# A two-block transformer kernel: the first attention moves between half chunks of the input projections, and sixteen modulation chunks become VectorE dot products

## The reference, cut to what matters

```python
# first block, one layer; x [256, 1024], ctx [256, 1024], float32
sh1, sc1, g1, sh2, sc2, g2 = split(silu(c) @ w_mod + b_mod, 6)       # w_mod [1024, 6144]
csh1, csc1, ...            = split(silu(c_ctx) @ w_mod + b_mod, 6)   # only the first two are used
hc = rmsnorm(ctx, n1) * (1 + csc1) + csh1;  kc, vc = hc @ w_in[:, KV]
h  = rmsnorm(x, n1) * (1 + sc1) + sh1
q, k, v, gb, gc, u, ga, gv = split(h @ w_in)                         # 4352 columns
y_attn = windowed_attention(rope(q), rope(k), v, kc, vc, sink) @ w_attn_out      # 8 heads of 64
y_conv = (gb * short_conv(gc * u)) @ w_conv_out
x = x + g1 * ((sigmoid(ga) * y_attn + sigmoid(gv) * y_conv) @ w_mix_out)
h2 = rmsnorm(x, n2) * (1 + sc2) + sh2
x = x + g2 * peer(h2, ...)      # per token 8 heads x 16 of 16384 experts: 128 rows of u and v gathered
# second block: two layers of attention and conv-gated FFN on x, then a norm
```

## Time and profile before

| | |
|---|---|
| median of three runs | 1725.31 us (1717.51 to 1727.1) |
| profiled execution | 1723.54 us, span 1721.3 us |
| PE busy | 1512.4 us (88%) |
| DVE, ACT, POOL busy | 1051.7, 771.6, 274.8 us |
| mean granted PE clock | 0.959 |
| DMA | 431.76 MB, mean 251 GB/s |

### The profile page before, as it was taken

The page is one execution under the profiler, slowest core; times in us unless marked ns, Lnnn a source line. Parts: engine busy times, 40 slices in busy tenths (PEclk is TensorE's granted clock), DMA queues, the critical chain, the costliest instruction groups (busy, mean ns, idle before and its releaser), DMA issues.

```text
span 1721.3 us, 22861 instructions
## 1 busy us (share of the span) xinstructions
PE 1512.4 (88%) x8364; PEld 1105.5 (64%) x8364; DVE 1051.7 (61%) x2111; ACT 771.6 (45%) x1648; POOL 274.8 (16%) x260
## 2 busy tenths in 40 slices
PE   7999998699888798877777779898999897899997
PEld 3897577554444233322222269788999886899997
DVE  4664335656666666766665557526777666367774
ACT  2644423244444344444444353536555546445553
POOL 0000000244344344344444200000000000000000
PEclk9999999899999999999999989789999998899998
DMA  8345344599999999999999924204555430145541
GB/s 359 138 157 182 137 172 147 234 405 420 419 419 420 420 420 420 420 420 419 420 420 420 392 89 160 99 30 147 190 174 192 165 128 26 74 172 172 193 172 73
DMA packets 59986, 431.76 MB, mean 251 GB/s; under 512 B 6784, under 2 KB 7296, under 8 KB 7552
## 3 DMA queue, kind: packets, MB, share of 16 engines
q0 software_dynamic: 36864, 268.45, 37.7%
q1 hardware_dynamic: 22320, 161.62, 26.0%
q10 hardware_dynamic: 720, 0.62, 0.1%
HBM read 429.62 MB, written 1.05 MB: 250 GB/s over the span
## 4 chain that ended last, share of the span: by engine, by line
PE 44%; DMA 23%; ACT 6%; DVE 6%; issue 2%; POOL 0%; ACTq 0%; POOLq 0%; DVEq 0%; SPq 0%
DMA arena<-in_peer_uv,experts 19%; PE banks L612 18%; PE banks L968 10%; PE banks L1074 7%; DMA tok_b<-in_peer_uv,experts 2%; DVE wlow L1527 2%; PE banks L854 2%; PE banks L644 1%; ACT diag L1347 1%; PE banks L828 1%; ACT scores L1255 1%; PE banks L666 1%; DVE arena L1912 1%; ACT whigh L1116 1%; ACT L1339 1%
## 5 line engine op out<-in xcount | busy, mean ns | idle before, releaser
L968 PE MATMUL banks<-arena,diag 128*128 128x512 f32 x824 | 402.0, 624 | 102.2 <-ACT diag L1347 101.6
L1912 DVE CUSTOM_DVE_ANT_0 arena<-arena,scores 128x1024 f32<-128x1024 f32 x206 | 252.5, 1226 | 191.4 <-DMA arena<-in_peer_uv,experts 189.6
L968 PEld LDWEIGHTS banks<-arena,diag 128*128 128x128 f32 x824 | 148.9, 194 | 342.0 <-ACT diag L1347 206.4
L1527 DVE TENSOR_TENSOR wlow<-wring,whigh 128x1024 fp32r<-128x1024 f32 x234 | 275.5, 1220 | 109.6 <-ACT whigh L1116 109.5
L1489 POOL DMA_INDIRECT arena<-in_peer_uv,experts x206 | 220.6, 1071 | 627.6 <-DVE experts L1876 322.3
L1116 ACT ACTIVATE whigh<-wring 128x1024 fp32r<-128x1024 f32 x234 | 233.8, 1048 | 140.3 <-DMA wring<-in_w_down 33.2
L612 PE MATMUL banks<-f_high,whigh 128*128 128x256 f32 x720 | 206.3, 287 | 17.2 <-DVE f_low L1563 11.8
L612 PE MATMUL banks<-f_low,whigh 128*128 128x256 f32 x720 | 205.2, 285 | 0.0
L612 PE MATMUL banks<-f_high,wlow 128*128 128x256 f32 x720 | 205.1, 285 | 0.0
L1339 ACT ACTIVATE dots<-dots 128x1 f32<-128x1 f32 x256 | 51.5, 201 | 302.2 <-DVE dots L1912 301.5
L612 PE MATMUL banks<-a_high,whigh 128*128 128x256 f32 x560 | 166.9, 298 | 14.2 <-DVE a_low L1535 7.9
(11 more groups left out here) (237 smaller groups left out, 2470.5 us busy)
## 6 DMA issues: line engine op xcount, KB each, us to landing
wring<-in_w_up SPq DMA_DIRECT2D x44, 1024.0 KB, 4.9
wring<-in_w_down SPq DMA_DIRECT2D x22, 1024.0 KB, 4.8
wring<-in_w_in SPq DMA_DIRECT2D x17, 1024.0 KB, 5.3
wring<-in_w_mod SPq DMA_DIRECT2D x16, 1024.0 KB, 4.8
wring<-in_w_qkv_a SPq DMA_DIRECT2D x12, 1024.0 KB, 4.9
arena<-in_w_mod SPq DMA_DIRECT2D x8, 1024.0 KB, 15.8
wring<-in_peer_w_q SPq DMA_DIRECT2D x8, 1024.0 KB, 7.3
wring<-in_w_mix_out SPq DMA_DIRECT2D x4, 1024.0 KB, 4.9
```

The source lines that it names most:

```text
L968: mm = nc.tensor.matmul(banks[:, 2 + 2 * b + half, :], diag[:, n % DIAGS, :], ring[n % RING][:, D + half * 512:D + (half + 1) * 512], star ...
L1527: V.tensor_tensor(low, w, high.bitcast(F32), ALU.subtract).then_inc(w_split, 1)
L1912: V.tensor_tensor_reduce(out=ring[n % RING][:, 0:D], in0=ring[n % RING][:, 0:D], in1=h2tok[:, b, :], scale=1.0, scalar=0.0, op0=ALU.mult, ...
```

## The change

The twelve modulation chunks of the attention and the four of the gather are gone from SP, PE and ACT. In their place the host lays the remaining 4096 columns of `w_mod` out by feature (`w_mod_t`: a row for each output feature) and `c` in 128 equal rows. POOL loads 32 tiles of 128 x 1024 (0.5 MB) into four buffers, and DVE multiplies each with the SiLU of the row of `c` and sums along it (`dot_tile`, one fused instruction, which leaves one column of `mod`): 24 tiles in the slots 7 to 30 of the new loop, 8 in the output products. `c` comes by a DMA of 0.5 MB among the early chunks; its SiLU is on ACT before the first norm's root.

The projections and the first attention are one loop of 32 slots on PE, ACT and DVE. A slot is half a chunk's product (24 matmuls); group n of the attention begins at slot 10 + 2n: score in that slot, turn two slots later, weigh four later, turn back six later. The scores of each group use banks 2 and 3 alone, and projections banks 0 and 1. The maxima become one fused instruction for each head, instead of two for scale and mask and one reduction. ACT now copies the gates plainly and makes their eight sigmoids after the loop. The first chunks of `w_qkv_a` wait until the last row of the gather has landed.

```diff
-MODS_PE = [i for i in range(MOD_TILES // 2) if i not in MODS_DVE]
-ROWS_1 = MODS_EARLY - len(MODS_DVE)
-ROWS_2 = 5 * KT // 2 - len(MODS_DVE)
-ROWS_3 = len(MODS_PE)
+MODS_PE = [i for i in range(MODS_EARLY) if i not in MODS_DVE]
+DOT_TILES = list(range(2 * KT, 3 * KT)) + list(range(4 * KT, 5 * KT)) + list(range(3 * KT, 4 * KT)) + list(range(5 * KT, 6 * KT))
+DOTS_MIXED = 3 * KT
+ROWS_1 = len(MODS_PE)
...
-MOD_ROWS = [88, 96, 104, 112]
...
+        dot_tiles = [region(4, 56 * T), region(4, 60 * T), hT[:, 0:4, :], hT[:, 4:8, :]]
+        dot_tiles = [t.rearrange("p k t -> p (k t)") for t in dot_tiles]
+        z_high, z_low = c_high[:, 0:4, :], c_low[:, 0:4, :]
+        o_high, o_low = c_high[:, 4:8, :], c_low[:, 4:8, :]
...
+        TURN, WEIGH, BACK = 2, 4, 6
+        FIRST_SLOT = 10
...
+                plan["at"] = {FIRST_SLOT + 2 * n: g for n, g in enumerate(groups)}
+                plan["slots"] = max(plan["at"]) + BACK + 2
...
-        add_mods(ROWS_1, ROWS_2)
...
+            load_mod(3)
+            sp.dma_start(c_row, a["c_rows"]).then_inc(c_row_in, 16)
+            for i in range(4, MODS_EARLY):
...
-                        sp.wait_ge(row_used, ROWS - 5)
+                        sp.wait_ge(row_in[(ROWS - 1) % RING], 16 * ((ROWS - 1) // RING + 1))
...
+            plan = plans[0]
+            for slot in range(plan["slots"]):
+                i, j = divmod(slot, 2)
+                if slot == 2:
+                    for which in range(2):
+                        key_value(which, 0)
+                        key_value(which, 1)
+                if i < 16:
+                    if j == 0 and i >= 2:
+                        pe.wait_ge(proj_read, i - 1)
+                    mm = tile_pair(i % 2, in_chunks[i + 1], high_low[0], (h_ready, 0) if slot == 0 else None, only=(j,))
+                    if j == 1:
+                        mm.then_inc(proj_made, 1)
+                if slot == 5:
...
+                if slot == FIRST_SLOT:
+                    pe.wait_ge(dup_read, 2)
+                    pe.wait_ge(kv_read, 3)
+                    pe.wait_ge(roped, 3)
+                at = plan["at"]
+                if slot - BACK in at and at[slot - BACK]["last"]:
+                    turn_heads(at[slot - BACK])
+                if slot - WEIGH in at:
+                    weigh(plan, at[slot - WEIGH])
+                if slot - TURN in at:
+                    turn_probs(at[slot - TURN])
+                if slot in at:
+                    score(plan, at[slot])
...
-                if n in MOD_ROWS:
-                    mod_chunk(ROWS_2 + MOD_ROWS.index(n))
...
+                    act.wait_ge(c_row_in, 16)
+                    nc.scalar.activation(c_row, c_row, ACT.Silu).then_inc(c_row_ready, 1)
...
+                if j == 1 and i < 16:
+                    if i == 1:
+                        act.wait_ge(kv_made, 1)
+                        copy(kraw, banks[:, 3, :]).then_inc(kv_read, 1)
+                        act.wait_ge(kv_made, 2)
+                        copy(kv_turned, banks[:, 6, :]).then_inc(kv_read, 1)
+                    dst, part = dests[i]
+                    act.wait_ge(proj_made, i + 1)
+                    copy(flat(dst[:, 2 * part:2 * part + 2, :]), banks[:, i % 2, :]).then_inc(proj_read, 1)
+                    if i == 3:
+                        for g in range(2):
+                            act.wait_ge(dup_made, g + 1)
+                            copy(kdup1[:, g, :], banks[:, 3 + g, :]).then_inc(dup_read, 1)
+                        act.wait_ge(kv_made, 3)
+                        copy(v1.rearrange("p b n -> p (b n)"), banks[:, 5, :]).then_inc(kv_read, 1)
+                    if i == 5:
+                        act.wait_ge(angles_ready, 1)
+                        nc.scalar.activation(sin2[:, :], tmp[:, 0, 0:T], ACT.Sin)
+                        nc.scalar.activation(cos2[:, :], tmp[:, 0, T:2 * T], ACT.Sin).then_inc(tables_ready, 1)
+                at = plan["at"]
+                if slot - BACK in at and at[slot - BACK]["last"]:
+
+                    act.wait_ge(z_made, 1)
+                    heads_out(plan, at[slot - BACK])
+                if slot - TURN in at:
+                    probs_out(at[slot - TURN])
+                if slot in at:
+                    exps(at[slot])
+                if j == 1 and i < 16:
+                    round_next()
+                if slot == 21:
+                    act.wait_ge(z_made, 1)
+                    copy(flat(z_high), flat(zconv[:, :, :])).then_inc(z_rounded, 1)
+            act.wait_ge(proj_read, 16)
+            for d in (sg_a, sg_c):
+                for part in range(4):
+                    tiles = flat(d[:, 2 * part:2 * part + 2, :])
+                    nc.scalar.activation(tiles, tiles, ACT.Sigmoid).then_inc(gates_ready, 1)
+
+            round_next()
...
+            for n, tile in enumerate(DOT_TILES):
+                if n == 0:
+                    pool.wait_ge(mod_rows, ROWS_1)
+                if n == 2:
+                    pool.wait_ge(h_ready, normed(1, 0))
+                if n >= 4:
+                    pool.wait_ge(tile_used, n - 3)
+                pool.dma_start(dot_tiles[n % 4], a["w_mod_t"][(tile - 2 * KT) * P:(tile - 2 * KT + 1) * P, :]
+                               ).then_inc(tile_in[n % 4], 16)
...
+            def dot_tile():
+
+
+                n = next(dot_next)
+                w = dot_tiles[n % 4]
+                dve.wait_ge(tile_in[n % 4], 16 * (n // 4 + 1))
+                V.tensor_tensor_reduce(out=w, in0=w, in1=c_row, scale=1.0, scalar=0.0, op0=ALU.mult, op1=ALU.add,
+                                       accum_out=mod[:, DOT_TILES[n], 0:1]).then_inc(tile_used, 1)
...
+                for j in range(heads):
+                    at = (j % each) * width
+                    ins = V.tensor_tensor_reduce(
+                        out=scores[:, n % 2, j * width:(j + 1) * width],
+                        in0=banks[:, g["score_bank"] + j // each, at:at + width], in1=g["mask"], scale=SCALE,
+                        scalar=LOWEST, op0=ALU.add, op1=ALU.max, accum_out=top[:, n % 2, j:j + 1])
+                ins.then_inc(score_read, 1)
...
+            for slot in range(5, plan["slots"]):
+                i, j = divmod(slot, 2)
+                if slot == 5:
+                    rope_key()
+                if slot == 6:
+                    rope_query(0)
+                    rope_query(1)
+                at = plan["at"]
+                if slot - BACK - 1 in at and at[slot - BACK - 1]["last"]:
+                    low_out(plan, at[slot - BACK - 1])
+                if slot - WEIGH in at and at[slot - WEIGH]["last"]:
+                    dve.wait_ge(tables_ready, 1)
+                    normalise(at[slot - WEIGH])
+                if slot in at:
+                    maxima(at[slot])
+                if j == 1 and i < 16:
+                    low_next()
+                if slot == 9:
+                    dve.wait_ge(roped, 3)
+                    angles()
+                if slot == 16:
+                    conv_middle()
+                if slot == 17:
+                    conv_left()
+                if slot == 18:
+                    conv_right()
+                if slot == 20:
+                    conv_out()
+                if slot == 23:
+                    low_conv()
+                if 7 <= slot < 7 + DOTS_MIXED:
+                    dot_tile()
...
+            dve.wait_ge(tile_used, DOTS_MIXED)
+            mixed = mod[:, 2 * KT:5 * KT, 0]
+            step.link(V.tensor_tensor(mixed, mixed, vcol[:, V_BMOD + 2 * KT:V_BMOD + 5 * KT], ALU.add))
             dve.sem_inc(mod_ready, 1)
             step.link(gains(2, 4, 0, V_N2))
 
 
             for g in range(8):
                 dve.wait_ge(mix_made, g + 1)
+                dve.wait_ge(gates_ready, g + 1)
                 sl = slice(2 * (g % 4), 2 * (g % 4) + 2)
                 if g < 4:
                     V.tensor_tensor(flat(merged[:, sl, :]), banks[:, g, :], flat(sg_a[:, sl, :]),
                                     ALU.mult).then_inc(mix_read, 1)
+                    dot_tile()
+                    dot_tile()
...
+    arrays["w_mod_t"] = np.ascontiguousarray(inputs["w_mod"][0][:, 2 * D:].T)
+    arrays["c_rows"] = np.ascontiguousarray(np.tile(inputs["c"], (P, 1)))
...
```

More of the change, by code:

```diff
@@ L98 @@
 C_END = C_MASK + 10 * P
+ALIGN = 8
 V_C = 0
@@ L461, in build @@
         len_of_ring = [0]
-        mod_chunks, in_chunks = [], []
-        def add_mods(first, last):
-            for p in range(first, last):
-                mod_chunks.append(add(chunk_of(a["w_mod"], MODS_PE[p]), (mod_rows, p + 1), split=False))
-        def mod_bank(p):
-            if p >= ROWS_2:
-                return 6
-            return 7 if ROWS_1 <= p else p % 2
+        in_chunks = []
         in_order = [1, 0] + list(range(2, len(W_IN_CHUNKS)))
@@ new lines, in _, with exps @@
+                dests += [(d, part) for part in range(4)]
+            def exps(g):
+                width = g["blocks"] * P
```

(10 more changed lines are left out.)

468 lines of the change are left out of this document (232 added, 236 removed).

## The result

The changed kernel takes 1659.2 us (median of 4 runs, 1653.3 to 1663.7), the kernel before 1721.4 (4 runs, 1717.3 to 1727.1): ratio 0.9635, 95% interval 0.9607 to 0.9663. It is 62 us faster; I had said 50.5, and my range ended at 1665. The forecast of 1675 counted from 1725.3, the median of the three runs that I had seen, and the kernel before has 1721.4 in the four runs here. So 3.9 of the 15.8 us between 1675 and 1659.2 are that base, and 11.7 are gain that I had not forecast. The profiled execution took 1661.6 (span 1659.8).

The account below looks back on a forecast made before the run. PE bounds projections and first attention, almost half of the latter's PE work not attention; DMA bounds the gather. Gains 46.9 - 8.1 + 10.0 + 3.2 = 52.0, less 1.5 for hops, 50.5 us: forecast 1675, range 1665 to 1692.

Parts of the forecast that it names:

- Modulation leaves PE, cover, stalls: Projections and first attention: modulation off PE -45.1 us, waits covered -3, new stalls +3.3; gain given as 46.9.
- my two small terms: Projections and first attention: about 3 us of waits at the stage's ends go, 3.3 us of stalls come.
- The one wait: First attention group: PE could transpose at 102 us but waits 2 to 3 us for late exponentials.
- The output products become DVE's: Output products: 12.4 us to the first merge, then 27.5 on DVE, 39.9 against 31.8; 8.1 us given back.
- The head, the tiles' DMAs: Early chunks and tile loads: the added load of c, its SiLU and 32 tile loads cost nothing.
- The gather stage: Gather: four chunks leave it, each worth one row of 2.48 us; -10.0 us.
- the signs: What would show the forecast right; in the gather an unchanged period of 2.5 and a length 10 us shorter.
- The end of the gather: Gather's end: the next projection's first chunks are issued after the last row, so the sums' copy starts 3.2 us earlier.
- Semaphore hops: Some forty new changes between product kinds: 1.5 us taken off the gain.
- The splits did not fall behind: Mixed stage rival: PE waits for weight splits, 2 us per pair over eight pairs, 1691; chance 0.15.
- the gather's gain came: Gather rival: the gain does not come and the late issue costs what it saves, 1688; chance 0.07.
- the clock: Mixed stage rival: PE at half clock, +74 us, about 1749; chance 0.03 together with anything else that loses.

Follow-up runs that it names:

- e12: The changed kernel with seven sigmoids before the last half chunk, eight dot tiles moved into the mixed slots, and the angles in slot 6, not 9: 1641.3 us.
- e6: The changed kernel with seven of the eight sigmoids moved ahead of the last half chunk: 1650.4 us.
- e7: The changed kernel with the last eight dot tiles moved out of the output products, into the pairs of slots with attention: 1649.4 us.
- e5: The changed kernel with four 1 MB loads of w_mod put back into the gather, read by nothing: 1666.4 us.
- e2: The changed kernel without its eight unused floats, so all buffers behind them start 32 bytes lower: 1665.5 us.
- e1: The kernel before with only eight unused floats (32 bytes a partition) put ahead of its buffers: 1707.7 us.
- e4: The changed kernel with the next projection's first three loads issued five rows ahead of the gather's end again: 1659.0 us.
- e8: The changed kernel with the first attention moved behind the last half chunk (first slot 32 instead of 10): 1677.7 us.
- e11: The changed kernel with seven sigmoids moved ahead of the last half chunk and the last eight dot tiles moved among the mixed slots: 1649.2 us.

## Why the prediction was wrong, step by step

- **Modulation leaves PE, cover, stalls (46.9):** near the 47.7 measured, partly by luck. The terms that I listed, -45.1 - 3 + 3.3, make 44.8 and not 46.9; no row gives the 2.1 between them. The windows from 46 us on have PE busy 45.2 us less (187.5 before, 142.3 after), which is my 45.1, and idle 2.5 us less (6.1 before, 3.6 after), where my two small terms together gave 0.3 more. The projections before had 3.0 us of idle time of their own, which I did not count. The one wait was predicted as 2 to 3 us near 102 and is 2.17 before 104.62; e12 removed it, and the loss of clock behind it, which my term did not hold.
- **The output products become DVE's (8.1 given back):** right, 8.7. The chain that I gave for the first merge (12.4 us) was right in length, but not in what bounds it: e6 shows that the sigmoids hide a late load of about the same end. e7 shows the rest, 17.5 us without dots where I had 27.5 - 9.8 = 17.7.
- **The head, the tiles' DMAs (0):** right. The first projection matmul starts at 45.6, and DVE waited once for a tile, 1.59 us.
- **The gather stage (-10.0): the step that failed.** I wrote that "a row takes 2.48 us" and in the signs "an unchanged period of 2.5". So I priced four rows fewer and held the period of the other 256 fixed; the pad in the diff stood in my sum at nothing, without a reason. The four chunks are worth what I said (9.5 in e5). But the period fell to 2.44, because 32 unused bytes put the buffers on a multiple of 256: 10.7 us by e2, 11.2 by e1. With 11 for it, the sum of the gain is 61.5, against 62.2 measured; counted from 1721.4 that is 1660.
- **The end of the gather (-3.2):** right in the trace, 3.8 in e4; the times can't confirm it.
- **Semaphore hops (1.5 taken off):** 3.1 went behind the gather, but that stretch varies by 11 us between executions of the same instructions, so nothing can be said of this term.
- **The rivals:** the splits did not fall behind (e7 bears even 8 dots more); the gather's gain came; the clock was 0.99 in the mixed stage, with 1.00 everywhere but behind the one wait (0.89 from 95 to 110), and e8 shows half speed for the attention's pieces alone. The gather's rate is no part of any rival: I had none for a faster row.

## What to carry to other kernels

Price every line of a diff that moves an address, not only those that move work: here one stage is bound by DMA for 650 us, and a pad of 32 bytes gave 1.6% of its rate, 11 us. Work in small pieces with a dependent chain (attention) is best laid between long products even when PE could do it alone: the waits are covered and the clock is kept, and in e8's trace each was about half of what the other order lost. Take work off the engine that ends a stage by name: the sigmoids beside a late load were worth 3 us, the dots on DVE's chain 7.5.

## What the runs showed of the hardware that I had not expected

- Gathered rows of 8 KB into SBUF (the on-chip memory in which the buffers lie): 427 GB/s with buffers that start at a multiple of 256 bytes of a partition, 421 at 64 or 128 beyond one, 419 to 420 at 224.
- One wait of 2.17 us of PE was followed by some 3.5 us at half speed (e11), and the same wait by none in e2, e4, e6 and e7. One of 7.2 us ahead of transposes, scores and weighings brought the granted clock to 0.50, and it stayed there for some 25 us of unbroken work of that kind: transposes of 8 blocks took 1.92 to 1.97 us there, 1.09 in the earlier trace rows.
- The stretch behind the gather, with the same instructions, took 709.4 to 720.5 us in the profiled executions of the changed kernel, e4, e7, e11 and e12.
